# Loading the expert weights of a mixture-of-experts decoder step in 2 MB transfers over pairs of ring slots

## What is computed

```python
logits = x2d @ w_router + b_router
top_vals, top_idx = lax.top_k(logits, 4);  gates = softmax(top_vals)
# for each expert e, over the tokens that chose it:
gu = xb @ w_gate_up[e] + b_gate_up[e]          # 1024 -> 2048
g, u = minimum(gu[:, :1024], 7), clip(gu[:, 1024:], -7, 7)
hid = (u + 1.0) * (g * sigmoid(1.702 * g))
out = hid @ w_down[e] + b_down[e]              # 1024 -> 1024
y[token] += gate * out
```

## Time and profile before

| | |
|---|---|
| median of 3 runs | 1552.32 us (1551.21 to 1552.47) |
| span of the profiled execution, first to last instruction | 1546.4 us |
| median less that span | 5.9 us |
| PE busy | 1282.3 us (83% of the span) |
| DVE, ACT, POOL busy | 347.7, 260.4, 70.2 us |
| DMA | 526.65 MB, mean 341 GB/s |
| HBM read, written | 507.39 MB, 18.87 MB |

### The profile page before, as it was taken

One profiled execution on the slowest core, in us unless ns is written; L12 is line 12 of the kernel. 1 busy time (PEld: TensorE's weight loads), 2 busy tenths in 40 slices (PEclk: granted clock), 3 DMA queues, 4 the chain that ended last, 5 costly groups with the idle time before them and its releaser, 6 DMA issues.

```text
span 1546.4 us, 19222 instructions
## 1 busy us (share of the span) xinstructions
PE 1282.3 (83%) x6721; PEld 512.7 (33%) x6722; DVE 347.7 (22%) x661; ACT 260.4 (17%) x439; POOL 70.2 (5%) x104
## 2 busy tenths in 40 slices
PE   8997787875696989988899888899888878887875
PEld 3444554553444322322223222233222222222222
DVE  0003546465554010012101100100100010001006
ACT  0003556565321011010000000000000000000000
POOL 0000000000000000000000000000000000000003
PEclk9999899996595999989899999999999999999997
DMA  9055898997113999999999999799999999999965
GB/s 388 23 191 175 254 325 299 346 349 309 42 66 146 373 418 418 417 416 418 418 418 416 418 418 419 286 417 416 418 418 418 416 417 418 419 417 416 418 278 170
DMA packets 127322, 526.65 MB, mean 341 GB/s; under 512 B 14720, under 2 KB 14848, under 8 KB 93344
## 3 DMA queue, kind: packets, MB, share of 16 engines
q1 hardware_dynamic: 116080, 496.95, 80.3%
q0 software_dynamic: 5936, 20.71, 4.1%
q10 hardware_dynamic: 5280, 8.65, 1.5%
HBM read 507.39 MB, written 18.87 MB: 340 GB/s over the span
## 4 chain that ended last, share of the span: by engine, by line
PE 32%; DMA 16%; SPq 12%; DVE 5%; issue 2%; ACT 1%; POOL 0%; ACTq 0%; POOLq 0%
DMA arena<-in_w_gate_up 15%; PE psum L1536 15%; PE psum L1552 12%; SPq L225 12%; PE psum L1527 2%; PE psum L1542 1%; DVE arena L1639 1%; DVE arena L1635 1%; DVE arena L1631 1%; DVE arena L1632 1%; ACT arena L1597 1%; PE psum L1572 1%; PE psum L1427 0%; PE psum L1584 0%; SPq L1461 0%
## 5 line engine op out<-in xcount | busy, mean ns | idle before, releaser
L1536 PE MATMUL psum<-arena 128*64 128x512 f32 x2112 | 478.8, 601 | 33.1 <-DMA arena<-in_w_gate_up 33.0
L1552 PE MATMUL psum<-arena 128*64 128x512 f32 x1056 | 277.3, 685 | 22.6 <-ACT arena L1597 22.6
L1536 PEld LDWEIGHTS psum<-arena 128*64 128x64 f32 x2112 | 143.7, 138 | 367.5 <-issue 270.9
L1631 DVE TENSOR_SCALAR arena<-psum 128x512 f32<-128x512 f32 x33 | 22.8, 692 | 864.5 <-PE psum L1536 864.5
L1552 PEld LDWEIGHTS psum<-arena 128*64 128x64 f32 x1056 | 82.6, 157 | 197.6 <-issue 164.5
L1595 ACT ACTIVATE arena<-arena 128x512 f32<-128x512 f32 x33 | 20.8, 630 | 570.9 <-DVE arena L1631 570.9
L599 PE MATMUL psum<-arena 128*128 128x128 f32 x512 | 75.3, 287 | 25.7 <-DMA arena<-in_cache_sb_k 8.2
L1542 PE MATMUL psum<-arena 128*128 128x128 f32 x132 | 25.4, 323 | 74.6 <-DVE arena L1639 74.6
L282 PE MATMUL psum<-arena 128*128 128x512 f32 x192 | 85.8, 603 | 0.0
L506 ACT ACTIVATE arena<-psum 128x512 f32<-128x512 f32 x112 | 61.9, 574 | 82.2 <-PE psum L599 50.1
L599 PEld LDWEIGHTS psum<-arena 128*128 128x128 f32 x512 | 56.3, 144 | 41.3 <-issue 15.0
(11 more groups left out here) (192 smaller groups left out, 856.5 us busy)
## 6 DMA issues: line engine op xcount, KB each, us to landing
arena<-in_w_gate_up SPq DMA_DIRECT2D x256, 1024.0 KB, 20.2
arena<-in_w_down SPq DMA_DIRECT2D x128, 1024.0 KB, 23.2
arena<-in_cache_sb_k SPq DMA_DIRECT2D x64, 256.0 KB, 4.4
arena<-in_cache_diff_k SPq DMA_DIRECT2D x64, 256.0 KB, 8.2
arena<-in_cache_sb_v SPq DMA_DIRECT2D x64, 256.0 KB, 5.1
arena<-in_cache_diff_v SPq DMA_DIRECT2D x64, 256.0 KB, 6.7
arena<-in_w_in SPq DMA_DIRECT2D x8, 1536.0 KB, 20.4
expert_rows<-arena ACTq DMA_DIRECT2D x66, 128.0 KB, 6.1
```

The costliest lines, as they stand in the source:

```text
L1536: ins = nc.tensor.matmul(psum[64 * h:64 * h + 64, n, :], x_k, slot[k][:, col:col + 512], start=False, stop=(k == KD - 1))
L1552: ins = nc.tensor.matmul(psum[64 * h:64 * h + 64, 4, :], h_k, slot[s][:, col:col + 512], start=(k == 0), stop=(k == KD - 1))
L1631: nc.vector.tensor_scalar(gate_in, psum[:, 0, :], LIMIT, None, ALU.min).then_inc(gate_clamped, 1)
```

## The change

`load_weights` takes an even slot number and loads that slot and the next with one transfer of 2 MB: two blocks of `w_gate_up`, or four of `w_down`. There are 6 semaphores `w_loaded` in place of 12. PE waits at slots 0, 2, 4, 6 and at 8 and 10 for the pair. SP's loop waits until both slots of a pair are used before it issues the pair. In the decode attention the pair 0, 1 is issued where slot 1 was, and the pair 2, 3 where slot 3 was; the pairs 4, 5 and 6, 7 are issued when both of their slots are free. `w_used` stays one semaphore per slot, and the bias row is issued behind the first pair.

```diff
-        w_loaded = [sem(f"w_loaded{s}") for s in range(RING)]
+        w_loaded = [sem(f"w_loaded{s}") for s in range(RING // 2)]
...
         def load_weights(sp, e, s):
 
+            assert s % 2 == 0
             if s < KD:
-                src = a["w_gate_up"][0, bass.ds(e, 1), s * P:(s + 1) * P, :].rearrange("e p n -> (e p) n")
-                dst = slot[s]
+                src = a["w_gate_up"][0, bass.ds(e, 1), s * P:(s + 2) * P, :].rearrange("e (r p) n -> p (e r) n", p=P)
+                n = 2
             else:
                 j = s - KD
-                src = a["w_down"][0, bass.ds(e, 1), 2 * j * P:(2 * j + 2) * P, :].rearrange("e (r p) n -> p (e r) n", p=P)
-                dst = slot[s].rearrange("p (r n) -> p r n", r=2)
-            sp.dma_start(dst, src).then_inc(w_loaded[s], 16)
+                src = a["w_down"][0, bass.ds(e, 1), 2 * j * P:(2 * j + 4) * P, :].rearrange("e (r p) n -> p (e r) n", p=P)
+                n = 4
+            dst = ring[:, s * SLOT:(s + 2) * SLOT].rearrange("p (r n) -> p r n", r=n)
+            sp.dma_start(dst, src).then_inc(w_loaded[s // 2], 16)
...
                 for s in (0, 4, 5, 1, 6, 7, 2, 3):
                     if s < 4:
                         past_used(sp, DEC_B, s)
-                        load_weights(sp, 0, s)
+                        if s % 2 == 1:
+                            load_weights(sp, 0, s - 1)
                     else:
                         load_pages(sp, DEC_B - 1, s, before, True)
...
-                for s in range(4, 8):
+                for s in (4, 6):
                     past_used(sp, DEC_B, s)
+                    past_used(sp, DEC_B, s + 1)
                     load_weights(sp, 0, s)
...
-                for s in range(8, RING):
-                    sp.wait_ge(projected, 5)
+                sp.wait_ge(projected, 5)
+                for s in range(8, RING, 2):
                     load_weights(sp, 0, s)
...
-                    for s in range(RING):
+                    for s in range(0, RING, 2):
                         sp.wait_ge(w_used[s], done)
+                        sp.wait_ge(w_used[s + 1], done)
                         load_weights(sp, e, s)
...
-                        pe.wait_ge(w_loaded[k], loaded)
+                        if k % 2 == 0:
+                            pe.wait_ge(w_loaded[k // 2], loaded)
...
-                        if r == 0:
-                            pe.wait_ge(w_loaded[s], loaded)
+                        if k % 4 == 0:
+                            pe.wait_ge(w_loaded[s // 2], loaded)
```

## The result

| | before | after |
|---|---|---|
| median, us | 1551.76 (4 runs, 1550.67 to 1552.47) | 1558.68 (4 runs, 1556.64 to 1559.76) |
| ratio, 95% interval | | 1.0053 [1.0037, 1.0069] |
| the same two kernels, a later comparison | 1549.23 (25 runs) | 1557.07 (12 runs), ratio 1.0043 [1.0029, 1.0057] |
| span of the profiled execution, us | 1546.4 | 1558.0 (its device time 1559.76) |

The change costs 6.7 to 8.2 us of 1551 by the two ratios, with intervals from 4.5 to 10.7. (A ratio is estimated from all runs and is not the quotient of the two medians: 1557.07 / 1549.23 would be 1.0051.

A forecast was written before the change was run, and what follows sets the result against it. The prediction took the expert stage to be bound by bytes at 417 to 418 GB/s. Terms 1.7 + 3.3 + 1.74 - 0.6 gave +6.1 us on a median of 1552.3: 1558.4 us, range 1553.5 to 1562.5.

The forecast's parts named there:

- The bound: In the expert stage, time is bound by bytes moved at 417 to 418 GB/s, not by how busy PE is.
- Term 1: At the stage's first reload, the pair waits for slot 1 instead of slot 0: +1.7 us, bounds +1.4 to +2.12.
- Term 2: Restart at the two-item expert: one slot more work after the landing and one before release, +3.49 us, taken as 3.3.
- Term 3: At the end, two slots of PE work instead of one follow the last landing of w_gate_up: +1.74 us.
- Term 4: Over 31 experts, 186 fewer transfers at no more than 0.007 us an end: -0.6 us, bounds -1.3 to 0.
- The rival by which ends give back 10 us: Ends of transfers cost 0.036 us or more each, so halving their number makes the kernel faster: 1549 us, chance 0.10.
- the partial one: Ends of transfers cost between 0.019 and 0.036 us each, giving about 1554 us; chance 0.16.
- the one on alternating rows: Reading two 8 KB rows 1 MB apart per partition slows w_gate_up by 22 us: 1580 us, chance 0.07.
- Step 5: In the steady state, later waits and releases are covered by a queue some 20 us deep: no cost.
- The margin before the pair 8, 9: At 520 to 530 us, only some 3 us spare before that pair is freed; DMA share below 1 would refute the forecast.
- Step 6: Loading expert 0 in the changed order during the attention, landed before 380 us and needed at 500: cost 0.
- The reference to the median: The trace's span of 1546.4 us was put 5.9 us below the median, and the same difference applied to the median.

The follow-up runs named there:

- experiment 8: The kernel before, unchanged, run again for a second trace; 1550.92 us for 1550.97.
- experiments 1 and 2: The kernel before: in 1, SP reloads only when both slots of a pair are used (ratio 1.0037); in 2, PE waits until both have landed (1.0028).
- Experiment 3: The changed kernel with each pair issued as two 1 MB transfers, a semaphore each, PE waiting on both; 1558.01 us for 1549.5 of the kernel before.
- experiment 4: The changed kernel with slots 0, 1, 6 and 7 single and the rest in pairs; 1553.38 us for 1549.5 of the kernel before.
- experiment 5: The changed kernel with only slots 2, 3 and 4, 5 left as 2 MB pairs, the rest single; 1551.25 us for 1550.97 of the kernel before.
- experiment 7: The kernel before with only slots 0 to 7 of expert 0 issued in the change's order, in 1 MB transfers; 1550.61 us for 1550.97.

## Why the prediction was right

The forecast was 1558.4 us, +6.1 on the median of before; the two ratios give +8.2 [5.7, 10.7] and +6.7 [4.5, 8.8]. The stretches of the expert stage, in us, from both traces of each kernel (landings are where PE starts on the last slot or pair of `w_gate_up`):

| from | to | before | before again | changed | changed again |
|---|---|---|---|---|---|
| first matmul on `w_gate_up` | first reload | 3.9 | 3.6 | 5.6 | 5.3 |
| first reload | last landing of the two-item expert | 467.9 | 467.4 | 470.6 | 467.6 |
| that landing | restart | 17.1 | 18.8 | 22.3 | 22.3 |
| restart | last landing of all | 499.2 | 500.5 | 499.4 | 500.3 |
| last landing | end of its matmuls | 1.9 | 1.9 | 3.7 | 3.7 |
| sum | | 990.1 | 992.2 | 1001.6 | 999.1 |

The second traces differ by 6.9 us, which is terms 1 to 3. The first differ by 11.5: 2.7 more from the dry stretch behind the bias step, and 1.7 from PE's clock in the item before the restart.

**The bound** was right. The plateau is 417 to 418 GB/s in every kernel here that writes all 128 partitions, and from the restart to the last landing before (499.2, and 500.5 in its second trace) and after (499.4, 500.3) need the same time.

**Term 1, the first reload:** taken at 1.7 within 1.4 to 2.12. From the first matmul of line 1536 to the reload, before has 3.9 and 3.6 us in its two traces, after 5.6 and 5.3: +1.7. The cause is as written, slot 1's release in place of slot 0's, but the 1.7 was reached otherwise: I took 2.12 for the slot from one trace and 0.4 off for fuller starts, and the slot itself was 1.7 (in experiment 8, 508.33 - 506.64). Whether the starts were fuller isn't shown: the stretch behind them is 467.6 against 467.4 and 467.9.

**Term 2, the restart:** 3.49 us for the issue, and 3.47 was found between traces with an equal clock. The traces of experiments 1 and 2 each hold one of its halves, 1.8 and 1.7 us. The 0.2 us that I took off for fuller starts can't be told from nothing.

**Term 3, the end:** 1.74. From the last landing to the end of the `w_gate_up` matmuls before took 1495.22 - 1493.29 = 1.93 us (experiment 8), after 1504.16 - 1500.51 = 3.65: +1.72. What followed was shorter in the trace of after, 7.09 us for 8.78, which is the clock that I had left as 1.7 either way.

**Term 4, the ends of transfers:** I took -0.6 with -1.3 as its bound. Experiment 3 has all 1 MB transfers and the changed kernel's time, so the gain is nothing that these runs can see; its interval can't tell 0.6 us from 0. The stretches give no sign of it either: from the first reload to the landing, and from the restart to the last landing, experiment 3 has 467.1 and 499.4 us, and the changed kernel in no trace less than 467.6 and 499.4. The rival by which ends give back 10 us is out, the partial one (0.019 us an end, 3.5 us in all) has no room in these stretches, as is the one on alternating rows: 8 KB rows 1 MB apart moved at the old rate.

**Step 5, "the queue is some 20 us deep and 3.5 us less still leaves it full",** is what failed, at a place that I had not looked at. The depth holds for PE's ordinary turn. Behind the bias step it does not (SP of before; line 1572 of before and line 1578 of the changed kernel are that step's matmuls):

```profile
729.30 13.72 SPq L225 DMA_DIRECT2D arena<-in_w_down  x4
753.37 0.34 SPq L225 DMA_DIRECT2D arena<-in_w_gate_up  x1
```

```profile
737.80 8.16 PE L1572 MATMUL psum<-arena 32*64 32x512 f32 x12 [2.40 <-ACT arena L1609]
```

```profile
742.18 10.76 PE L1578 MATMUL psum<-arena 32*64 32x512 f32 x12 [2.40 <-ACT arena L1615]
```

SP of before had its last `w_down` issued at 743.0 and issued the next reload at 753.37 us, with the rate held. In the first trace of the changed kernel it was 740.3 and 763.14, a pause of 22.9 us, since the pair needs slot 1 as well, PE began both slots at a granted clock of 0.50 (755 to 760 us), and the step's matmuls took 10.76 us for 8.16. That lost 3.4 us at 760 (5 x (1 - 134/418)). In the second trace the pause was 762.64 - 743.17 = 19.5 us and lost 0.3; experiment 3, with the same waits, read 357 GB/s there and lost 0.7. The stretch in the table is longer by 2.7 us in the one and by nothing in the other. So the pairs bring the queue to the edge there; that PE's clock then decides whether it runs dry fits the three traces, and no run varied it alone.

The margin before the pair 8, 9, which I had put at 3 us and given no price, is a second weak place, but not one that cost the changed kernel anything these traces show. Where slot 0 is single and 8, 9 a pair (experiment 4), the pair went out 1013.96 - 991.10 = 22.9 us behind the restart; with all of them single it was 18.1 us (1007.64 - 989.51) and 20.1, in experiment 5 19.9. In the changed kernel the restart waits for slot 1 as the pair waits for slot 9, so the distance stays:

```profile
1020.61 3.81 SPq L227 DMA_DIRECT2D arena<-in_w_down  x2
```

That is 19.5 us behind the restart at 1001.15, and 21.0 in the second trace, and from the restart to the last landing both kernels need the same time. With terms 1 to 3 and the bias step the sum is 1.7 + 3.5 + 1.7 + 0 to 3, or 6.9 to 9.9 us, against the 6.7 and 8.2 measured. The forecast of 6.1 left out that 0 to 3 and took off 0.6 for the ends that nothing shows; both lie within the intervals. The lower end of the sum is 1.4 + 3.2 + 1.74 - 1.3 = 5.0, not the 4.8 that I wrote.

**Step 6, expert 0,** at zero is borne out within 2.5 us either way (experiment 7).

**The reference to the median** was loose. I put 5.9 us between span and median. The device times of after lie 1.8 us above their spans, so some 4 us of it was that the profiled execution of before was short. The sum was made on the median, so the forecast is not touched by it.

## To carry to other kernels

In this kernel a queue that 1 MB transfers kept full gained nothing that could be seen from 2 MB ones, but the coarser waits cost wherever the queue starts from dry or ends. What can be tried elsewhere: count a slot's work once for each place where the first slot is freed or the last one lands, and look up each pause of the consumer, not only its ordinary turn, before calling a queue deep enough. If transfers are to be merged in a ring, merge in the middle of the order and leave single what is freed first after a pause and what lands last: experiment 5 did that at no cost and no gain beyond some 2 us. A pair far behind a single first slot waits one slot longer than it did (experiment 4). A clock that falls in another item moves single stretches by 2 to 3 us, so terms of that size are to be compared between stretches with an equal clock, or in a dozen runs.

## What the runs showed of the hardware

Loads of 0.5 MB into 64 of the 128 partitions moved at 227 GB/s with all engines busy (share 1.00), where the same 8 KB rows into 128 partitions moved at 422 to 426; 0.5 MB transfers of 4 KB rows into all 128 moved at 410. So the size of the transfer doesn't explain it, and the half of the partitions is what is left, at nearly half of the rate. The transfers for the two halves alternated in the queue, which did not make up for it. Whether two such streams side by side from two queues would was not tried.
